# Moving the start addresses of a kernel's large SBUF buffers

## What is computed

```python
h = rms_norm(x); proj = h @ w_in                       # recurrent branch, attention branch, gates
y_rnn  = (rg_lru(conv(rx)) * gelu(rgate)) @ w_rnn_out   # width 1344
y_attn = nsa(q, kc, vc, ks, vs, kw, vw, g) @ w_attn_out # 16 heads of 64
x = x + (sigmoid(mg_rnn) * y_rnn + sigmoid(mg_attn) * y_attn) @ w_out
x = x + (gelu(conv(gate)) * conv(val)) @ w_down         # FFN 0, 3072 wide
x = x + causal_attention(rope(q), rope(k), v) @ w_o     # layer 1, then FFN 1, 2816 wide
x = x + mla(x) @ w_o                                    # layer 2, then FFN 2, 2816 wide
out = rms_norm(x)
```

## The kernel before

| buffer | bytes | start before | start after |
|---|---|---|---|
| `w_raw` | 12288 | 0 | 896 |
| `w_high` | 24576 | 12288 | 13184 |
| `w_low` | 24576 | 36864 | 37760 |
| `small` | 8764 | 61440 | 202080 |
| `x` | 8192 | 70204 | 62336 |
| `h_high`, `h_low` | 8192 each | 78396, 86588 | 70528, 78720 |
| `r_high`, `r_low` | 11264 each | 94780, 106044 | 86912, 98176 |
| `ident_b`, `mask_b` | 256 each | 117308, 117564 | 0, 256 |
| `rstd` | 1024 | 117820 | 109440 |
| `stats` | 1856 | 118844 | 210844 |
| `arena` | 91616 | 120700 | 110464 |

## Time and profile before

### The profile page before, as it was taken

One profiled execution on the slowest core, in us unless ns is written; L12 is line 12 of the kernel. 1 busy time (PEld: TensorE's weight loads), 2 busy tenths in 40 slices (PEclk: granted clock), 3 DMA queues, 4 the chain that ended last, 5 costly groups with the idle time before them and its releaser, 6 DMA issues.

```text
span 1249.0 us, 25297 instructions
## 1 busy us (share of the span) xinstructions
PE 1186.1 (95%) x9597; PEld 1151.2 (92%) x9597; DVE 929.3 (74%) x1581; ACT 679.9 (54%) x1184; POOL 17.4 (1%) x14
## 2 busy tenths in 40 slices
PE   5997998999999999999999999999999799999996
PEld 5997898999999999999899899999998689999996
DVE  5777789467777898888768667877775776876765
ACT  5766764334455575555554456655565645655552
POOL 1000000000001000000000010000000000000000
PEclk9998998999999999999999999999998899999998
DMA  6574544432225476655465026766654314666650
GB/s 213 184 215 133 160 145 122 131 119 68 68 71 167 165 227 199 185 186 185 139 198 165 21 85 199 223 200 189 198 152 136 102 35 135 194 212 185 185 184 34
DMA packets 52780, 190.95 MB, mean 153 GB/s; under 512 B 5984, under 2 KB 5984, under 8 KB 52576
## 3 DMA queue, kind: packets, MB, share of 16 engines
q1 hardware_dynamic: 52416, 188.77, 48.6%
q10 hardware_dynamic: 288, 1.12, 0.2%
HBM read 188.82 MB, written 1.05 MB: 152 GB/s over the span
## 4 chain that ended last, share of the span: by engine, by line
PE 81%; DVE 10%; ACT 4%; DMA 3%; issue 2%; SPq 0%; DVEq 0%; ACTq 0%
PE bank L499 23%; PE bank L501 22%; PE bank L500 22%; DMA w_raw<-weight_stream 3%; DVE w_low L1367 2%; PE bank L592 2%; PE bank L603 1%; ACT w_high L995 1%; PE bank L591 1%; PE bank L617 1%; PE bank L616 1%; PE bank L615 1%; PE bank L507 1%; DVE arena L1605 1%; PE bank L508 1%
## 5 line engine op out<-in xcount | busy, mean ns | idle before, releaser
L1367 DVE TENSOR_TENSOR w_low<-w_raw,w_high 128x1024 fp32r<-128x1024 f32 x356 | 434.3, 1224 | 158.1 <-ACT w_high L995 154.5
L995 ACT ACTIVATE w_high<-w_raw 128x1024 fp32r<-128x1024 f32 x356 | 375.1, 1058 | 301.4 <-PE bank L501 228.9
L499 PE MATMUL bank<-h_high,w_high 128*128 128x256 f32 x1824 | 521.3, 286 | 18.3 <-DVE h_low L1405 11.7
L500 PE MATMUL bank<-h_low,w_high 128*128 128x256 f32 x1824 | 511.6, 280 | 0.0
L501 PE MATMUL bank<-h_high,w_low 128*128 128x256 f32 x1824 | 511.4, 280 | 0.0
L499 PEld LDWEIGHTS bank<-h_high,w_high 128*128 128x128 f32 x1824 | 346.7, 190 | 22.2 <-issue 13.0
L500 PEld LDWEIGHTS bank<-h_low,w_high 128*128 128x128 f32 x1824 | 346.3, 190 | 0.6
L501 PEld LDWEIGHTS bank<-h_high,w_low 128*128 128x128 f32 x1824 | 346.5, 190 | 0.0
L499 PE MATMUL bank<-r_high,w_high 128*128 128x256 f32 x866 | 245.3, 283 | 14.4 <-ACT arena L1196 7.3
L500 PE MATMUL bank<-r_low,w_high 128*128 128x256 f32 x866 | 242.2, 280 | 0.0
L501 PE MATMUL bank<-r_high,w_low 128*128 128x256 f32 x866 | 242.1, 280 | 0.0
(11 more groups left out here) (206 smaller groups left out, 1194.9 us busy)
## 6 DMA issues: line engine op xcount, KB each, us to landing
w_raw<-weight_stream SPq DMA_DIRECT2D x356, 512.0 KB, 4.0
small<-small_in ACTq DMA_DIRECT2D x1, 1065.5 KB, 8.3
x<-x_in SPq DMA_DIRECT2D x4, 256.0 KB, 6.0
out<-arena SPq DMA_DIRECT2D x4, 256.0 KB, 2.5
small<-small_in ACTq DMA_DIRECT2D x1, 30.0 KB, 4.3
```

Source lines behind the costliest of these rows:

```text
L499: mm(out_ap, wh, high, start=start, stop=False, skip_group_check=True)
L500: mm(out_ap, wh, low, start=False, stop=False, skip_group_check=True)
L995: fn(w_high[:, c % RING, :], w_raw[:, c % RAW, :], ACT.Copy).then_inc(high_ready, 1)
L1367: v.tensor_tensor(w_low[:, c % RING, :], w_raw[:, c % RAW, :], f(w_high[:, c % RING, :]), ALU.subtract).then_inc(low_ready, 1)
```

## The change

Two bf16 tables of 256 bytes and a filler of 384 bytes come first, so that everything behind them starts 896 bytes later; `small` and `stats`, whose sizes are no multiples of 1024, move behind the others. No instruction is added, removed or moved: every engine has the same instructions with the same shapes and waits in the same order, at other addresses. All lines below L153 have a number higher by one.

```diff
+        ident_b = sb("ident_b", [P, P], BF16)
+        mask_b = sb("mask_b", [P, P], BF16)
+        sb("line_fill", [P, 96])
         w_raw = sb("w_raw", [P, RAW, D])
         w_high = sb("w_high", [P, RING, D], F32R)
         w_low = sb("w_low", [P, RING, D], F32R)
-        small = sb("small", [P, N_SMALL])
         x = sb("x", [P, DT, S])
         h_high = sb("h_high", [P, DT, S], F32R)
         h_low = sb("h_low", [P, DT, S], F32R)
         r_high = sb("r_high", [P, RT, S], F32R)
         r_low = sb("r_low", [P, RT, S], F32R)
-        ident_b = sb("ident_b", [P, P], BF16)
-        mask_b = sb("mask_b", [P, P], BF16)
         rstd = sb("rstd", [P, S])
+        arena = sb("arena", [P, 22904])
+        small = sb("small", [P, N_SMALL])
         stats = sb("stats", [P, 464])
-        arena = sb("arena", [P, 22904])
```

## The result

The changed kernel takes 1271.7 us (median of 4 runs, 1270.1 to 1275.9), the kernel before 1252.7 us beside it: ratio 1.0168, 95% interval 1.013 to 1.0207. It is slower by some 20 us (19.0 between the medians, 21.6 between the two traced spans), and outside the range of the prediction. The profiled execution took 1272.4 us, with a span of 1270.6 us against 1249.0 before.

A forecast was written before the change was run, and what follows sets the result against it. The prediction took the distance between TensorE's 8070 back-to-back fp32r matmuls to bound the kernel. Every term was 0, so the sum was 0 against the profiled 1250.91 us: forecast 1251 us, range 1222 to 1266.

The forecast's parts named there:

- What bounds the kernel: TensorE: time is 8070 fp32r matmuls times the distance between them, 113.3 or 117.8 ns; 53 to 90 us are lost there.
- (a) on VectorE and ScalarE: Activation buffers moved from supposed odd-word starts to multiples of 1024: 0 us on these engines, 1 us either way.
- (a) on TensorE: Matmul operands moved from supposed odd-word starts to multiples of 1024: 0 us, from -35 to +12.
- The upper bound: TensorE matmuls: the short third of the stream also goes to 117.8 ns, 12 us more, 1263 us.
- The slow-side rival: TensorE: operands at the same residue make streams fall to 117.8 ns more often; 12 us more, 1263 us; chance 0.21.
- the further loss: TensorE: both streams in step lose another 4.5 ns on all matmuls, 36 us more; chance 0.03 of the 0.21.
- the rival of the short level: TensorE streams fall to 113.3 ns more often: 24 us less if all do, 1227 us, or 1239 if half; chance 0.17.
- The odd start is the loss: TensorE: odd starts touch 17 pieces of 64 bytes instead of 16; aligning saves 37 us, 1214 to 1225 us; chance 0.18.
- Levels that vary by chance: TensorE: no effect beyond the mix of matmul levels that varies anyway, 1247 to 1256 us; chance 0.44.
- (b) the DMA: Weight buffers' start moved from 128 to 0 modulo 1024: 0 us on weight transfers, from -7 to +4.
- the sign that the prediction named for a real DMA term: Weight loads: landings of 3.8 us or less, instead of 4.0, would show that aligned starts pay.
- The rivals the other way: TensorE gets faster: more matmuls at 113.3 ns (1227 us, chance 0.17) or odd starts cured (1214 to 1225 us, 0.18).

The follow-up runs named there:

- the first experiment: Changed kernel without its 384-byte filler, every buffer behind it starting 384 bytes earlier: 1274.7 us, ratio 1.0183 to the kernel before.
- the kernel at 192: Kernel before with 128 bytes added after `small`, putting `h` and `r` at distance 192 modulo 256 from the weights: 1239.2 us, ratio 0.9928.

## Why the prediction was wrong

*What bounds the kernel:* right. It is the distance in time between fp32r matmuls, and the two levels and the question whether addresses have a part in them were the right ones to look at.

*(a) on VectorE and ScalarE, 0 us:* right, 1223 and 2216 ns, 1057 ns. But my ground for it was void, since rows 8 and 9 compare starts that were all on 32-byte boundaries. What bears it out is that the moved buffers gave the same durations at every distance (L1367's form 1223 to 1224 ns, L995's 1057 to 1059 ns in all 18 traces).

*(a) on TensorE, 0 us:* **this is the step that failed.** It said "An aligned moving operand thus loses as much as an odd one" and took 0. It looked at the start of each operand by itself, and with the starts as they were no operand in the comparison was odd. The rows of before held one distance and its opposite: `h` or `r` moving over `w` at 64, and in rows 6 and 7 `w` moving over `h` or `r`, the same two buffers again. Swapping roles never brought them to a distance of 0, so those rows could not show what the change would do, and their agreement with rows 3 was no evidence for zero. The measured term is +27.7 us of matmul distance, +20 us of time: what the change alters for TensorE is the distance between the two starts, 64 to 0 modulo 256, and at 0 every matmul of an FFN takes 120.0 ns. I should have kept it as unknown to both sides.

*The upper bound, +12 us* "the long level everywhere", took the worst level seen for the worst there is. The new level is 2.2 ns above it.

*The slow-side rival* named the mechanism: both operands at the same residue, the state with more lost, FFN 1 paying most (it did, 10 of the 20 us). Its price was 12 us, where 27.7 of matmul distance were measured, because it kept to the levels in the trace; the further loss that it put at 4.5 ns and a chance of 0.03 is what came, with 2.2 ns over the long level. What no row spoke for was that equal residues are the bad case: the rival stated it as a guess, and the rival of the short level held the phase of two address streams for a possible gain.

*The odd start is the loss:* its premise was false, there was no odd start, so 17/16 of the columns has nothing to do with one. The rule on 16-byte lines had nothing to act on.

*Levels that vary by chance:* right as far as it goes. The kernel before ran between 1240.8 and 1258.3 us in 17 runs on one chip, and the two traces of distance 64 have different FFNs at the short level, FFN 1 in one and FFNs 0 and 2 in the other. Distance 0 shows one level in the FFNs of all four traces that have it for `h` and `r`, and its 12 runs in three kernels lie within 6 us (1270.1 to 1275.9). The change traded a mix of levels for the longest one seen.

*(b) the DMA, 0 us:* the sign that the prediction named for a real DMA term, landings of 3.8 us or less, did come, with 3.6 us; but it does not show one. Seven of the other traces with the weights at 128 modulo 256, as before the change, have landings of 3.7 us too (the first experiment is one), and in three more they are 3.9 to 4.2 us. The weight packets of 4096 bytes took 159 ns as a median in every trace, so the start shows no price per packet. The Trainium skill ("DMA: Bandwidth & Descriptors", How a descriptor splits into AXI transactions) has a transfer that does not start at a multiple of 256 bytes fetch the bytes below its start as well, which speaks of reads; for these writes into SBUF the traces do not bear it out. The 0.4 us by which landings fell against the trace of before is not explained.

*The rivals the other way* (more of the short level): not by this change. A distance of 192 comes nearest, with a triple of 346.6 ns against 349.5 for `h`.

## What to carry to other kernels

When a kernel lives on a back-to-back stream of fp32r matmuls, the start of the moving tile less the start of the stationary piece, modulo 256 bytes, is a setting worth 3% of the stream in this change (349.5 to 359.7 ns a triple) and 5% between the extremes here (341.8 to 359.8), and it changes whenever any buffer between the two changes its size. Count matmuls in a 100 us window of a busy loop, try a few fillers in steps of 32 or 64 bytes, and avoid 0, which was never better than 358.8 ns here; aligning everything to a large power of two is how one gets it. Read starts from the built program, since a sum of sizes misses the allocator's rounding.

## What the hardware showed that was not expected

- How long a matmul takes depends on how the start of its moving tile lies to that of the stationary pieces. The Trainium skill ("SBUF — State Buffer", Who interferes with whom) gives TensorE two independent read ports, one for the moving operand and one for weight loads, and says that it never waits on anyone. Read that way, the distance would do nothing. Here it moves a matmul from 113.9 to 120.0 ns on the mean, and does nothing at the 1.2 GHz level, 213.3 ns at distance 0 and at 64. The measurement decides; what in the memory does it was not seen.
- A matmul's time has levels that last for over 100 us and change at an interruption: 113.3 and 117.8 ns at distances of 64 and 192, 116.7 and 120.0 at 32, 120.0 alone at 0. What picks the level at a restart is open.
- A distance of 96 is as bad as 0 for `h` (359.5 ns), and the pattern isn't even about 128: 32 and 224 differ by 2 to 4 ns. With 512 columns moving the order turns round: a median of 227 ns in the four traces with both parts of `h` and of the weights at 0, 229 to 235 ns in the other 14. No rule for the form of the pattern came out of these runs.
- Open too: whether `arena` has a part in the 0.7% of the kernel at 192, since it moves along with the rest there.
